# The output-gate tiles of a sink attention, multiplied between its steps

## The chip, the cores and the metric

The kernel runs on one core of one Trainium2 chip. The metric is the device time of one execution in microseconds, as the median of several executions; lower is better. Engines are named as the profile names them: PE is TensorE (PEld its weight loads), DVE is VectorE, ACT is ScalarE, SP is SyncE, which issues the DMA transfers.

## The reference, cut to what matters

Two transformer blocks follow each other on 256 tokens of width 1024. The second one puts 16 meta tokens ahead (272 positions) and starts with a gated attention with a sink logit for each head; the part that the change touches is this:

```python
def attention_mixer(h, norm_w, w_in, q_norm_w, k_norm_w, sinks, w_out):
    u = rms_norm(h, norm_w) @ w_in
    q, k, v, gate = jnp.split(
        u, [ATTN_WIDTH, ATTN_WIDTH + ATTN_KV_WIDTH, ATTN_WIDTH + 2 * ATTN_KV_WIDTH], axis=-1)
    q = rms_norm(q.reshape(B, L, ATTN_HEADS, ATTN_HEAD_DIM), q_norm_w)
    k = rms_norm(k.reshape(B, L, ATTN_KV_HEADS, ATTN_HEAD_DIM), k_norm_w)
    o = banded_sink_attention(q, k, v, sinks)
    return (o * jax.nn.silu(gate)) @ w_out
```

There are 16 query heads of 64 and 2 key/value heads. Everything is fp32.

## The kernel before, in words

The kernel is a sequence of stages, each a block of instruction streams written out by hand for PE, DVE, ACT and SP. An engine runs its stream in order, streams wait for each other by counting semaphores, and all engines meet at the end of a block. Weights come as tiles of 128x1024 fp32 into a ring of four buffers (`load_tiles`, on SP). Each tile is split in two parts for the products: `make_high` (ACT, L172) rounds it, `make_low` (DVE, L184) takes the rest; both parts have two buffers. `tile_T` multiplies one tile into a PSUM bank with 16 matmuls on the high part (L219) and 8 on the low part (L223), each 128x128 by 272 columns.

The stages around the change, in order of time:

- `project_T` for `attn_t`: 19 tiles, one after another on PE. Tiles 0 to 7 are the queries, 8 and 9 the keys, 10 the values, and 11 to 18 the output gate. DVE copies products 0 to 10 out of PSUM; ACT takes the eight gate products out with Silu (L1738) into `T2[:, 10:18]`.
- `value_rows_stage`: three PE transposes of the values, copied out by DVE (L1717).
- `head_norm_stage`, the norm of each query and key head; `meta_attention_stage`, the attention of the 16 meta tokens.
- `sink_attention_stage`: 16 units, u = 0 to 15, each two heads of one query tile of 128; units 0 to 7 see 144 keys, units 8 to 15 see 272. PE runs, in step u: `scores(u+2)` (L1509), `values(u-1)` (L1534), `turn(u)` (L1521, which transposes the probabilities). DVE runs, in its step u: `peaks(u)` (L1558 to L1571, the scores with bias into SBUF and their maximum), `scale(u-1)` (L1577, L1579, L1582, the probabilities divided by their sum, which `turn(u-1)` waits for) and `store(u-3)` (L1589, the product of `values` times the gate, into `y2`). ACT runs `exps(u)` (L1609, L1612) and `copy_turned(u-1)` (L1620, L1623), which `values(u-1)` waits for. `values` has PSUM banks 6 and 7 in turn. In step 2 ACT and DVE also split the first two tiles of `attn_out`.
- `out_rows` for `attn_out`: ACT and DVE split `y2` in pairs of rows (L2516, L2524), PE multiplies (L2547).

The same kernel has a stage of this kind in its first block, `attention_stage`, where weight tiles are multiplied between the steps of an attention; there `store` is on ACT.

## Time and profile before

| | |
|---|---|
| median of the runs (lowest to highest), us | 2078.43 (2077.08 to 2081.27) |
| the profiled execution, us | 2075.18 |
| its span, first to last instruction, us | 2073.4 |
| busy in the span: PE, DVE, ACT | 87%, 61%, 42% |
| mean granted clock of TensorE | 0.904 of 2.4 GHz |

A window of the trace gives the busy time of each engine in a stretch, and PEclk, the granted share of the full clock: 1.00 is 2.4 GHz and 0.50 is 1.2 GHz. A timeline gives start, duration, engine, line, operation and its operands, and in brackets how long the engine had been idle before and who released it. A fp32 matmul of this kernel shows as two records, so "x4" of L1509 are two matmuls.

### The profile page before, as it was taken

How to read it: one execution, taken by the hardware profiler on the slowest of the kernel's cores; microseconds unless marked ns; L12 is line 12 of the kernel's file. 1: busy time of each engine (PE TensorE's matmuls, PEld its weight loads, DVE VectorE, ACT ScalarE, POOL GpSimd, SP SyncE). 2: the span in 40 equal slices, each digit the busy share in tenths (PEclk: the TensorE clock that was granted, in tenths of full speed). 3: DMA queues.
4: the chain of work that ended last, by engine and by line, in shares of the span. 5: the costliest groups of instructions: out<-in, count | busy, mean ns of one | idle time of the engine just before them, and what ended most of it. 6: DMA issues, size and time to landing. Idle time of an engine off the chain costs nothing. (4 is left out here: it accounts for less than half of the span.)

```text
span 2073.4 us, 33110 instructions
## 1 busy us (share of the span) xinstructions
PE 1810.1 (87%) x11956; PEld 1612.6 (78%) x11956; DVE 1256.3 (61%) x2175; ACT 873.7 (42%) x1655; POOL 40.4 (2%) x24
## 2 busy tenths in 40 slices
PE   6899878899999986679999996869869887888878
PEld 6887768899999975668888885844568885888876
DVE  4544555589894459985555555546357634556554
ACT  3334543244444445545555554324334342234333
POOL 0000000000000000000000000000013200000000
PEclk9979989999999997769999998876889996999989
DMA  5422244455555530005666654410224430000014
GB/s 175 161 97 67 72 133 143 142 173 182 182 167 188 182 122 0 0 31 193 192 192 192 192 193 136 153 41 1 71 76 149 144 101 0 1 1 1 1 39 145
DMA packets 62765, 229.62 MB, mean 111 GB/s; under 512 B 6976, under 2 KB 7232, under 8 KB 62544
## 3 DMA queue, kind: packets, MB, share of 16 engines
q1 hardware_dynamic: 62672, 228.36, 34.1%
q8 instruction: 61, 1.00, 0.2%
q14 instruction: 32, 0.26, 0.0%
HBM read 227.29 MB, written 1.05 MB: 110 GB/s over the span
## 5 line engine op out<-in xcount | busy, mean ns | idle before, releaser
L981 DVE TENSOR_TENSOR tile_low<-weights,tile_high 128x1024 fp32r<-128x1024 f32 x252 | 307.4, 1223 | 248.0 <-ACT tile_high L971 243.0
L184 DVE TENSOR_TENSOR tile_low<-weights,tile_high 128x1024 fp32r<-128x1024 f32 x154 | 191.7, 1251 | 249.1 <-ACT tile_high L172 195.2
L971 ACT ACTIVATE tile_high<-weights 128x1024 fp32r<-128x1024 f32 x252 | 266.3, 1057 | 174.8 <-issue 173.7
L219 PE MATMUL banks<-parts,tile_high 128*128 128x272 f32 (+1 forms) x1904 | 270.7, 297 | 36.0 <-PEq L264 18.0
L219 PEld LDWEIGHTS banks<-parts,tile_high 128*128 128x128 f32 x1904 | 255.2, 200 | 43.6 <-issue 31.4
L172 ACT ACTIVATE tile_high<-weights 128x1024 fp32r<-128x1024 f32 x169 | 177.3, 1055 | 234.5 <-PE banks L219 100.1
L1025 PE MATMUL banks<-parts,tile_high 128*128 128x256 f32 x2048 | 268.6, 284 | 7.0 <-PEq L907 7.0
L1025 PEld LDWEIGHTS banks<-parts,tile_high 128*128 128x128 f32 x2048 | 256.9, 193 | 7.2 <-issue 7.2
L1312 PE MATMUL banks<-tile_high,parts 128*128 128x512 f32 x1024 | 255.1, 391 | 2.2 <-ACT parts L1292 2.2
L1312 PEld LDWEIGHTS banks<-tile_high,parts 128*128 128x128 f32 x1024 | 193.7, 189 | 42.7 <-issue 2.4
L1245 PE MATMUL banks<-rows 128*128 128x128 f32 x512 | 107.8, 378 | 48.6 <-ACT rows L1232 48.6
L1030 PE MATMUL banks<-parts,tile_low 128*128 128x256 f32 x1024 | 145.7, 285 | 3.0 <-DVE tile_low L981 3.0
L1245 PEld LDWEIGHTS banks<-rows 128*128 128x128 f32 x512 | 93.4, 274 | 63.0 <-issue 53.7
L223 PE MATMUL banks<-parts,tile_low 128*128 128x272 f32 (+1 forms) x952 | 140.3, 290 | 2.2 <-POOL tile_low L184 0.7
L1312 PE MATMUL banks<-tile_low,parts 128*128 128x512 f32 x512 | 137.7, 391 | 0.0
L1030 PEld LDWEIGHTS banks<-parts,tile_low 128*128 128x128 f32 x1024 | 132.6, 193 | 4.6 <-DVE tile_low L981 3.8
L1049 ACT ACTIVATE big<-banks 128x256 f32 (+1 forms) x127 | 49.0, 386 | 202.0 <-PE banks L1030 202.0
L223 PEld LDWEIGHTS banks<-parts,tile_low 128*128 128x128 f32 x952 | 127.8, 194 | 5.2 <-POOL tile_low L184 5.2
L1312 PEld LDWEIGHTS banks<-tile_low,parts 128*128 128x128 f32 x512 | 96.7, 189 | 20.2
L1232 ACT ACTIVATE rows<-rows 128x128 f32<-128x128 f32 x256 | 81.8, 390 | 72.3 <-DVE rows L1186 72.3
L2547 PE MATMUL banks<-tile_high,parts 128*128 128x512 f32 (+1 forms) x288 | 76.5, 413 | 10.9 <-ACT tile_high L172 9.5
L1186 DVE TENSOR_TENSOR rows<-const,rows 128x512 f32<-128x512 f32 x128 | 84.1, 714 | 1.4 <-PE banks L1245 1.1
(336 smaller groups left out, 2261.1 us busy)
## 6 DMA issues: line engine op xcount, KB each, us to landing
weights<-in_peer_u SPq DMA_DIRECT2D x128, 512.0 KB, 3.5
weights<-in_peer_v SPq DMA_DIRECT2D x128, 512.0 KB, 3.5
weights<-in_dn_qkv SPq DMA_DIRECT2D x32, 512.0 KB, 4.2
weights<-in_in_t SPq DMA_DIRECT2D x19, 512.0 KB, 3.6
weights<-in_attn_t SPq DMA_DIRECT2D x19, 512.0 KB, 3.5
weights<-in_in_m SPq DMA_DIRECT2D x16, 512.0 KB, 3.7
weights<-in_wq SPq DMA_DIRECT2D x16, 512.0 KB, 4.3
weights<-in_dn_z SPq DMA_DIRECT2D x16, 512.0 KB, 3.5
```

What stands on the lines that cost most here:

```text
L172: k.nc.scalar.activation(k.high[:, m % 2, :], k.ring.view(n), ACT.Copy).then_inc(*k.high_made.up())
L184: unit.tensor_tensor(k.low[:, m % 2, :], k.ring.view(n), k.high[:, m % 2, :].bitcast(F32), ALU.subtract).then_inc(*k.low_made[engine].up())
L219: ins = nc.tensor.matmul(out, high[:, c, :], rhs(c)[part], start=part + c == 0, stop=False)
L223: ins = nc.tensor.matmul(out, low[:, c, :], rhs(c)[0], start=False, stop=c == chunks - 1)
L971: k.nc.scalar.activation(k.high[:, (s + j) % 2, :], k.ring.buf[:, j % RING, :], ACT.Copy).then_inc(k.high_made.sem, 1)
L981: k.nc.vector.tensor_tensor(k.low[:, (s + j) % 2, :], k.ring.buf[:, j % RING, :], k.high[:, (s + j) % 2, :].bitcast(F32), ALU.subtract).th ...
L1025: ins = nc.tensor.matmul(ps[:, j, 0:S], high[:, c, :], x[:, c, :], start=part + c == 0, stop=False)
L1030: ins = nc.tensor.matmul(ps[:, j, 0:S], low[:, c, :], k.pair(S)[0][:, c, :], start=False, stop=c == KC - 1)
L1186: return nc.vector.tensor_tensor(out, iota.unsqueeze(1).broadcast_to([P, Q, NKEY]), choice(o, i, g, 0, Q).unsqueeze(2).broadcast_to([P, Q, ...
L1232: nc.scalar.activation(first[:, g % A, q, :], first[:, g % A, q, :], ACT.Copy, scale=choice(2, i, g, q, 1)).then_inc(scaled.sem, 1)
L1245: ins = nc.tensor.matmul(ps[:, g, q * P:(q + 1) * P], first[:, g % A, q, :], second[:, g % B, q, :], start=True, stop=True)
L1312: ins = nc.tensor.matmul(ps[:, 2 * tt + half, :], c[:, j % STAGES, tt * P:tt * P + P], v[:, half, :], start=head and j + part == 0, stop=t ...
```

## The change

The `attn_t` projection ends after tile 10. The eight gate tiles become a group `attn_g` of the ring, and each of the first eight steps of the sink attention multiplies one of them into PSUM bank 7; `values` keeps to bank 6 until these are through. Their first two splits are made in `value_rows_stage`, the others and the first two of `attn_out` in the attention, one in a step. ACT copies each gate product out, and in its step 10 applies Silu to all eight at once (2176 elements in a row). DVE's `store` becomes a plain copy. It belongs to step u-2 and stands ahead of `scale`. `out_rows` multiplies the rows by the gate, on DVE, ahead of splitting them (`open_gate`).

```diff
--- before.py
+++ after.py
@@ -38,6 +38,7 @@
 PH, TOPK = 8, 16
 NKEY = 128
 AH = 16
+N_ATTN = 11
 DNK, DNV = 8, 16
 CH = 64
 AHEAD = 2
@@ -119,7 +120,9 @@
     for j in range(NKEY):
         r.add(d["peer_v"][j])
     r.align()
-    for name in [n for n in ("attn_t", "attn_out", "dn_qkv", "dn_ba", "dn_z", "dn_out") if n in d]:
+    group("attn_t", d["attn_t"][0:N_ATTN])
+    group("attn_g", d["attn_t"][N_ATTN:])
+    for name in ("attn_out", "dn_qkv", "dn_ba", "dn_z", "dn_out"):
         group(name, d[name])
     k.tiles["end"] = len(r.slots)
@@ -1480,7 +1483,13 @@
     AK, GATE = 8, 10
     scored, masked, peaked, exped = k.start("att_scored", "att_masked", "att_peaked", "att_exped")
     scaled, turned, unturned, summed = k.start("att_scaled", "att_turned", "att_copied", "att_valued")
-    stored, stats = k.start("att_stored", "att_stats")
+    stored, stats, gated = k.start("att_stored", "att_stats", "gate_made")
+    fills = AH // 2
+    gate_tile = lambda i: k.tiles["attn_g"] + i
+    ahead = [gate_tile(i) for i in range(AHEAD, fills)] + list(early(k, "attn_out"))
+    high, low = k.pair(L)
+    fill = ps[:, 7, 0:L]
+    value_bank = lambda u: 6 + u % 2 if u > fills else 6
     units = [(tt, a) for tt in range(NT) for a in range(AH // 2)]
     keys = lambda tt: META + (tt + 1) * P
     soft, pt = k.soft2, k.pt2
@@ -1525,13 +1534,15 @@
             def values(u):
                 tt, a = units[u]
                 pe.wait_ge(*unturned.at(u + 1))
-                if u >= 2:
-                    pe.wait_ge(*stored.at(u - 1))
+                if u == fills + 1:
+                    pe.wait_ge(*gated.at(fills))
+                elif u:
+                    pe.wait_ge(*stored.at(u - 1 if u > fills else u))
                 tiles = key_tiles(tt)
                 for j in range(2):
                     g = (2 * a + j) // 8
                     for i, (_, n) in enumerate(tiles):
-                        ins = nc.tensor.matmul(ps[HD * j:HD * j + HD, 6 + u % 2, 0:P], k.v2[0:n, i, g * HD:(g + 1) * HD],
+                        ins = nc.tensor.matmul(ps[HD * j:HD * j + HD, value_bank(u), 0:P], k.v2[0:n, i, g * HD:(g + 1) * HD],
                                                pt[0:n, u % 2, i, j, :], start=i == 0, stop=i == len(tiles) - 1)
                 ins.then_inc(*summed.up())
@@ -1540,6 +1551,10 @@
             for u in range(len(units) + 1):
                 if u + 2 < len(units):
                     scores(u + 2)
+                if u < fills:
+                    if u:
+                        pe.wait_ge(*gated.at(u))
+                    tile_T(pe, k, gate_tile(u), fill, lambda c: (high[:, c, :], low[:, c, :]))
                 if u:
                     values(u - 1)
                 if u < len(units):
@@ -1586,19 +1601,17 @@
                 tt, a = units[u]
                 dve.wait_ge(*summed.at(u + 1))
                 cols = slice(META + tt * P, META + tt * P + P)
-                nc.vector.tensor_tensor(k.y2[:, a, cols], ps[:, 6 + u % 2, 0:P], T[:, GATE + a, cols],
-                                        ALU.mult).then_inc(*stored.up())
-
-            for u in range(len(units) + 3):
+                nc.vector.tensor_copy(k.y2[:, a, cols], ps[:, value_bank(u), 0:P]).then_inc(*stored.up())
+
+            for u in range(len(units) + 2):
                 if u < len(units):
                     peaks(u)
+                if u >= 2:
+                    store(u - 2)
                 if 1 <= u <= len(units):
                     scale(u - 1)
-                if u == 2:
-                    for n in early(k, "attn_out"):
-                        make_low(dve, k, n)
-                if u >= 3:
-                    store(u - 3)
+                if 1 <= u <= len(ahead):
+                    make_low(dve, k, ahead[u - 1])
 
         @block.scalar
         def _(act):
@@ -1628,17 +1641,23 @@
             for u in range(len(units) + 1):
                 if u < len(units):
                     exps(u)
+                if 1 <= u <= len(ahead):
+                    make_high(act, k, ahead[u - 1])
+                if 1 <= u <= fills:
+                    act.wait_ge(k.ring.used.sem, gate_tile(u - 1) + 1)
+                    nc.scalar.activation(T[:, GATE + u - 1, :], fill, ACT.Copy).then_inc(*gated.up())
                 if u:
                     copy_turned(u - 1)
-                if u == 2:
-                    for n in early(k, "attn_out"):
-                        make_high(act, k, n)
+                if u == fills + 2:
+                    act.wait_ge(*gated.at(fills))
+                    nc.scalar.activation(T[:, GATE:GATE + fills, :], T[:, GATE:GATE + fills, :],
+                                         ACT.Silu).then_inc(*gated.up())
 
 
 def meta_attention_stage(k):
 
     nc, ps, T = k.nc, k.ps, k.T2
-    AK, GATE = 8, 10
+    AK = 8
     pe_done, vec, exped = k.start("meta_product", "meta_vector", "meta_exped")
     m = META
     k.meta_soft, k.meta_turned = k.carve(k.mid, (AH, META), (AH, META))
@@ -1689,8 +1708,7 @@
             dve.wait_ge(*pe_done.at(2))
             done(nc.vector.tensor_copy(turned.rearrange("p h n -> p (h n)"), ps[0:m, 2, 0:AH * m]))
             dve.wait_ge(*pe_done.at(3))
-            done(nc.vector.tensor_tensor(k.y2[:, :, 0:m], ps[:, 3, 0:8 * m].rearrange("p (c n) -> p c n", c=8),
-                                         T[:, GATE:GATE + 8, 0:m], ALU.mult))
+            done(nc.vector.tensor_copy(k.y2[:, :, 0:m], ps[:, 3, 0:8 * m].rearrange("p (c n) -> p c n", c=8)))
 
         @block.scalar
         def _(act):
@@ -1715,6 +1733,13 @@
             for i, (_, n) in enumerate(spans):
                 dve.wait_ge(*turned.at(i + 1))
                 nc.vector.tensor_copy(k.v2[0:n, i, :], ps[0:n, i, 0:P]).then_inc(*copied.up())
+            for n in early(k, following):
+                make_low(dve, k, n)
+
+        @block.scalar
+        def _(act):
+            for n in early(k, following):
+                make_high(act, k, n)
 
 
 def second_block(k, stop):
@@ -1732,13 +1757,12 @@
     end_early(k, "attn_t")
     V = 10
 
-    def put(eng, i, src):
-        if i <= V:
-            return nc.vector.tensor_copy(k.vT2 if i == V else k.T2[:, i, :], src)
-        return nc.scalar.activation(k.T2[:, i - 1, :], src, ACT.Silu)
-    project_T(k, "attn_t", 19, L, (lambda i: "vector" if i <= V else "scalar", put), k.tiles["attn_out"] + RING)
+    project_T(k, "attn_t", N_ATTN, L,
+              (lambda i: "vector", lambda eng, i, src: nc.vector.tensor_copy(k.vT2 if i == V else k.T2[:, i, :], src)),
+              k.tiles["attn_g"] + RING)
     spans = [(0, META)] + [(META + tt * P, P) for tt in range(NT)]
-    value_rows_stage(k, spans)
+    value_rows_stage(k, spans, "attn_g")
+    end_early(k, "attn_g")
     if stop <= 22: return
 
     def apply_qk(c, wide):
@@ -1755,7 +1779,7 @@
     end_early(k, "attn_out")
     if stop <= 24: return
     out_rows(k, "attn_out", [(k.hm, 0, META, 0)] + [(k.h[:, tt, :], 2 + 2 * tt, P, META + tt * P) for tt in range(NT)],
-             k.y2, k.tiles["dn_qkv"] + RING)
+             k.y2, k.tiles["dn_qkv"] + RING, k.T2[:, 10:18, :])
     if stop <= 25: return
     deltanet(k, tiles, stop)
@@ -2494,12 +2518,12 @@
     peer(k, stop)
 
 
-def out_rows(k, name, tiles, x, prefetch):
+def out_rows(k, name, tiles, x, prefetch, gate=None):
 
 
     nc, ps, first = k.nc, k.ps, k.tiles[name]
     pairs, cols = x.shape[1] // 2, x.shape[2]
-    x_high, x_low, added = k.start("lhs_high", "lhs_low", "rows_added")
+    x_high, x_low, added, gated = k.start("lhs_high", "lhs_low", "rows_added", "lhs_gated")
     place = lambda q: slice(2 * (q % 4), 2 * (q % 4) + 2)
     high_x, low_x = k.pair(cols)
     with nc.Block() as block:
@@ -2513,16 +2537,26 @@
             for q in range(pairs):
                 if q >= 4:
                     act.wait_ge(k.ring.used.sem, first + 2 * (q - 4) + 2)
+                if gate is not None:
+                    act.wait_ge(*gated.at(q + 1))
                 nc.scalar.activation(high_x[:, place(q), :], x[:, 2 * q:2 * q + 2, :], ACT.Copy).then_inc(*x_high.up())
                 for half in range(2):
                     make_high(act, k, first + 2 * q + half)
 
         @block.vector
         def _(dve):
+            def open_gate(q):
+                if gate is not None and q < pairs:
+                    pair = x[:, 2 * q:2 * q + 2, :]
+                    nc.vector.tensor_tensor(pair, pair, gate[:, 2 * q:2 * q + 2, :], ALU.mult).then_inc(*gated.up())
+
+            open_gate(0)
+            open_gate(1)
             for q in range(pairs):
                 dve.wait_ge(*x_high.at(q + 1))
                 nc.vector.tensor_tensor(low_x[:, place(q), :], x[:, 2 * q:2 * q + 2, :],
                                         high_x[:, place(q), :].bitcast(F32), ALU.subtract).then_inc(*x_low.up())
+                open_gate(q + 2)
                 for half in range(2):
                     make_low(dve, k, first + 2 * q + half)
             dve.wait_ge(k.ring.used.sem, first + 2 * pairs)
```

Here is one step of DVE's stream in the units with 272 keys: in the order before, line L1577 to L1582 are `scale(u-1)`, L1589 is `store(u-3)`, and L1558 begins the next `peaks`. Names in brackets are the semaphores waited for.

```order
L1563 TENSOR_REDUCE small<-big 128x2 [waits att_stats,att_masked]
L1565 TENSOR_TENSOR small<-small,param 128x2 [waits att_stats]
L1568 TENSOR_TENSOR small<-param,small 128x2 [waits att_stats]
L1571 TENSOR_SCALAR small<-small 128x2 [waits att_stats]
L1577 TENSOR_TENSOR small<-small 128x2 [waits att_exped]
L1579 RECIPROCAL small<-small 128x2 [waits att_stats]
L1582 TENSOR_SCALAR big<-big,small 128x272 [waits att_stats]
L1582 TENSOR_SCALAR big<-big,small 128x272
L1589 TENSOR_TENSOR big<-banks,big 128x128 [waits att_valued]
L1558 SCALAR_TENSOR_TENSOR big<-big,banks 128x272 [waits att_turned,att_scored]
```

In the changed kernel `scale` is L1592 to L1597, `store` L1604.

```order
L1578 TENSOR_REDUCE small<-big 128x2 [waits att_stats,att_masked]
L1580 TENSOR_TENSOR small<-small,param 128x2 [waits att_stats]
L1583 TENSOR_TENSOR small<-param,small 128x2 [waits att_stats]
L1586 TENSOR_SCALAR small<-small 128x2 [waits att_stats]
L1604 COPY big<-banks 128x128 [waits att_valued]
L1592 TENSOR_TENSOR small<-small 128x2 [waits att_exped]
L1594 RECIPROCAL small<-small 128x2 [waits att_stats]
L1597 TENSOR_SCALAR big<-big,small 128x272 [waits att_stats]
L1597 TENSOR_SCALAR big<-big,small 128x272
L1573 SCALAR_TENSOR_TENSOR big<-big,banks 128x272 [waits att_turned,att_scored]
```

The store has moved from behind `scale` to ahead of it, and it is now that of unit u-2: its wait on `att_valued` is for the `values` that ran one step later than before.

PE's stream in the early steps, before: `values(u-1)` (L1534), `turn(u)` (L1521), `scores(u+3)` (L1509).

```order
L1534 MATMUL banks<-big 64x128 [waits att_stored,att_copied]
L1534 MATMUL banks<-big 64x128 x3
L1521 MATMUL banks<-const,big 16x128 [waits att_copied,att_scaled]
L1521 MATMUL banks<-const,big 16x128
L1521 MATMUL banks<-const,big 128x128 x2
L1509 MATMUL banks<-big 128x144 [waits att_masked]
L1509 MATMUL banks<-big 128x144
```

In the changed kernel (`values` L1545, `turn` L1530, `scores` L1518, a gate tile L222 and L226):

```order
L1545 MATMUL banks<-big 64x128 [waits att_stored,att_copied]
L1545 MATMUL banks<-big 64x128 x3
L1530 MATMUL banks<-const,big 16x128 [waits att_copied,att_scaled]
L1530 MATMUL banks<-const,big 16x128
L1530 MATMUL banks<-const,big 128x128 x2
L1518 MATMUL banks<-big 128x144 [waits att_masked]
L1518 MATMUL banks<-big 128x144
L222 MATMUL banks<-parts,tile_high 128x272 [waits high_made,gate_made]
L222 MATMUL banks<-parts,tile_high 128x272 x15
L226 MATMUL banks<-parts,tile_low 128x272 [waits low_made_vector]
L226 MATMUL banks<-parts,tile_low 128x272 x7
```

The 24 matmuls of a tile stand between `scores` and the next `values`, and wait for the copy of the gate product before (`gate_made`) and for the tile's splits.

ACT's stream in its step 10 has the Silu with a table load on either side; L1633 and L1636 are `copy_turned(9)`, L1622 begins `exps(11)`.

```order
L1633 ACTIVATE big<-banks 16x256 [waits att_valued,att_turned]
L1636 ACTIVATE big<-banks 128x512 [waits att_meta_copied]
L1653 ACT_TABLE_LOAD
L1653 ACTIVATE big<-big 128x2176 [waits gate_made]
L1622 ACT_TABLE_LOAD
L1622 ACTIVATE small<-small 128x2 [waits att_peaked]
```

The load and Silu of before stood at the first gate product of the projection; now they stand between a `copy_turned` and the next `exps`, and the load for Exp follows.

## Rows read from the trace of the kernel before

**Rows 1.** Windows; busy time by engine, PEclk is the granted share of 2.4 GHz

```profile
1301.46:1361.43 59.97, 59.97 (x456) 59.75 (x456) 24.70 (x28) 21.55 (x25) 0.00 (x0) 0.95 0.53 167
1410.00:1440.00 30.00, 28.54 (x104) 14.61 (x106) 19.80 (x84) 11.64 (x48) 0.00 (x0) 0.50 0.00 1
1440.00:1458.60 18.60, 16.87 (x110) 10.04 (x108) 15.10 (x55) 9.97 (x35) 0.00 (x0) 0.98 0.01 1
1458.60:1475.18 16.58, 11.88 (x49) 7.37 (x49) 2.14 (x9) 4.80 (x13) 0.00 (x0) 0.58 0.00 0
```

**Rows 2.** Timeline of PE in the projection; start and duration in us

```profile
1301.46 3.97 PE L219 MATMUL banks<-parts,tile_high 128*128 128x272 f32 x16 [6.21 <-PEq L264]
...
1307.04 2.39 PE L219 MATMUL banks<-parts,tile_high 128*128 128x272 f32 x16
...
1358.27 2.16 PE L219 MATMUL banks<-parts,tile_high 128*128 128x272 f32 x16
```

**Rows 3.** Timeline of PE, the attention's first instructions and its step 4

```profile
1394.41 2.31 PE L1509 MATMUL banks<-big 64*128 64x144 f32 x12 [0.94 <-PEq L1648]
...
1416.49 0.85 PE L1509 MATMUL banks<-big 64*128 64x144 f32 x4
1417.44 2.54 PE L1534 MATMUL banks<-big 16*64 16x128 f32 x8
1419.90 1.02 PE L1521 MATMUL banks<-const,big 128*16 128x128 f32 x4
```

**Rows 4.** Timeline of DVE, step 6 of its loop, scale(5)

```profile
1418.89 0.15 DVE L1577 TENSOR_TENSOR small<-small 128x2 f32<-128x2 f32 x1
...
1419.28 0.50 DVE L1582 TENSOR_SCALAR big<-big,small 128x144 f32<-128x144 f32 x2
```

**Rows 5.** Timeline of PE, turn(12), values(12), turn(13), full clock

```profile
1453.99 0.82 PE L1521 MATMUL banks<-const,big 128*16 128x128 f32 x6
...
1455.91 1.95 PE L1534 MATMUL banks<-big 16*64 16x128 f32 x12 [0.43 <-ACT big L1623]
1457.79 0.82 PE L1521 MATMUL banks<-const,big 128*16 128x128 f32 x6
```

**Rows 6.** Timeline of PE, values(13), turn(14), values(14)

```profile
1459.70 2.33 PE L1534 MATMUL banks<-big 16*64 16x128 f32 x12 [1.09 <-ACT big L1623]
1461.96 1.45 PE L1521 MATMUL banks<-const,big 128*16 128x128 f32 x6
1464.50 3.39 PE L1534 MATMUL banks<-big 16*64 16x128 f32 x12 [1.09 <-ACT big L1623]
```

**Rows 7.** Timeline of DVE, scale(15), store(13), store(14), store(15)

```profile
1460.78 0.16 DVE L1577 TENSOR_TENSOR small<-small 128x2 f32<-128x2 f32 x1 [1.98 <-ACT big L1612]
...
1461.18 0.63 DVE L1582 TENSOR_SCALAR big<-big,small 128x272 f32<-128x272 f32 x2
1462.07 0.29 DVE L1589 TENSOR_TENSOR big<-banks,big 128x128 f32<-128x128 f32 x1 [0.26 <-PE banks L1534]
1467.93 0.29 DVE L1589 TENSOR_TENSOR big<-banks,big 128x128 f32<-128x128 f32 x1 [5.57 <-PE banks L1534]
1473.79 0.29 DVE L1589 TENSOR_TENSOR big<-banks,big 128x128 f32<-128x128 f32 x1 [5.57 <-PE banks L1534]
```

**Rows 8.** Timeline, the turning of the value rows and what follows

```profile
1362.47 0.68 DVE L1717 COPY big<-banks 16x128 f32<-16x128 f32 x3 [5.64 <-PE banks L1711]
1363.44 0.75 ACT L1444 ACTIVATE big<-big 128x272 f32<-128x272 f32 x2 [1.58 <-PEq L1706]
```

**Rows 9.** By line: table load and split of one tile; duration ns min/median/max

```profile
L1738 ACT ACT_TABLE_LOAD  x1: 1283/1283/1283, 1340.6 to 1340.6; - x1
...
L172 ACT ACTIVATE tile_high<-weights x8: 1045/1060/1060, 1339.5 to 1406.3; 128x1024 fp32r<-128x1024 f32 x8
...
L184 DVE TENSOR_TENSOR tile_low<-weights,tile_high x8: 1218/1226/1227, 1406.4 to 1501.9; 128x1024 fp32r<-128x1024 f32 x8
```

**Rows 10.** Windows in the first block's attention, whose weight tiles lie between steps

```profile
225.00:230.00 5.00, 4.00 (x32) 3.76 (x32) 3.41 (x4) 2.96 (x7) 0.00 (x0) 1.00 0.15 43
```

More of the change, by code:

```diff
@@ L1699, in _, with value_rows_stage @@
             nc.scalar.activation(soft, soft, ACT.Exp).then_inc(*exped.up())
-def value_rows_stage(k, spans):
+def value_rows_stage(k, spans, following):
     nc, ps = k.nc, k.ps
```

## The prediction

> **What bounds the kernel now.** I read the windows by stage first. In the projection PE is busy all 59.97 us and its clock is full but for the beginning [rows 1]; DVE and ACT have less than half of that to do. So each tile costs PE its own time. The first runs at half clock and takes 1307.04 - 1301.46 = 5.58 us; the next seventeen take (1358.27 - 1307.04) / 17 = 3.01 us each [rows 2]. The attention, from 1394.41 [rows 3] to the end of the last store at 1473.79 + 0.29 = 1474.08 [rows 7], takes 79.7 us. It has three phases. From 1410 to 1440 PE is busy 28.54 of 30 us, at the half clock throughout; then 16.87 of 18.6 us at 0.98 of the full clock; then, once no scores are left, 11.88 of 16.58 us and mostly at half clock again [rows 1]. So it is PE's for most of the time, and its clock is set by something other than PE being busy.
>
> The timelines say what stands between PE's instructions. `turn(u)` needs `scale(u)` of DVE. Before the change this is nearly free: scale(5) runs from 1418.89 to 1419.78 [rows 4] while PE is in values(3), and turn(4) starts at 1419.90 [rows 3] with its own scale long done. DVE is one unit ahead of PE. That lead is what I follow below.
>
> **The change, part by part.**
>
> *The projection.* Eight tiles of 3.01 us go, on an engine that does nothing else: **-24.1 us**. The copies or Silus of their products lay beside PE. No transfer is late for it: DMA has 0.53 of its time taken there [rows 1].
>
> *The value rows.* Two tiles are now split there. DVE ends its copies at 1363.15 and the next stage starts at 1363.44 [rows 8]. ACT's two splits (1.06 us each) lie beside the copies for the most part, DVE's two (1.23 each) [rows 9] come behind the copies: **+2.5 us**, with no cover, since the block ends with them.
>
> *The attention's steps with a tile.* Here the first thing is the new wait. PE runs values(u-1), then turn(u). turn(u) waits for scale(u). DVE now has store(u-1) in its stream ahead of scale(u), and store(u-1) waits for values(u-1). So after each `values` PE has to wait for a store and a whole scale. That chain cannot be hidden by anything in PE's stream, because values(u-1) and turn(u) are neighbours in it. Its length, from rows: 0.04 from the end of `values` to the store (1459.70 + 2.33 = 1462.03 to 1462.07 [rows 6, 7]); the store 0.29 (as a plain copy perhaps a little less; I keep 0.29, and half of it would take 0.15 off each step); 0.05 to the next instruction; scale, 1418.89 to 1419.78, 0.89 with 144 keys [rows 4], or 1460.78 to 1461.81, 1.03 with 272 keys [rows 7]; 0.15 from there to `turn` (1461.96 [rows 6]). That is **1.42** and **1.56 us** in every step.
>
> The tile itself is 24 dense matmuls, 3.01 at full clock or 5.58 at half. No row has a dense tile within this attention, but the first block's has: over 225 to 230 PE is busy 4.00 of 5 us with gaps, and the clock stays at 1.00 [rows 10]. So I take the full clock once the first tile is through. The short instructions shrink with it: `values` is 1.95 at full and 3.39 at half clock for the same 12 records [rows 5, 6], a factor of 0.575, `turn` 0.82 against 1.45. For 144 keys this makes scores 0.85 to 0.48, values 2.54 to 1.46, turn 1.02 less its overlap to 0.55 [rows 3]. A step is then 0.48 + 3.01 + 1.46 + 1.42 + 0.55 = **6.9 us**. In it DVE has 0.89 + 0.29 + 1.23 for a split + some 1.6 for `peaks`, 4.0 in all, and ACT less: both are covered, and the splits are ready a step ahead.
>
> The start: three scores 2.31 [rows 3], the first tile 5.58 at half clock, turn and scores 0.95 each, the second tile 3.01, values 1.46, the wait 1.42: turn(1) starts 15.7 us into the stage. turn(7) is six steps on, 57.1. From there turn to values is 1.92 (1453.99 to 1455.91 [rows 5]; it is `copy_turned`, which no tile covers any more), values 1.46, the wait 1.56: turn(8) starts at **62.0**.
>
> *The steps without a tile.* Now turn, copy, values, store, scale, turn is one chain with nothing beside it. At full clock: 1.92 + 1.95 + 1.56 = 5.43 us, where the step before the change was 1457.79 - 1453.99 = 3.80 [rows 5]. At half: 2.54 (1461.96 to 1464.50) + 3.39 + 1.56 = **7.49** [rows 6]. Which clock? In a step of 5.43 PE works 1.95 + 0.82 and some 0.73 for scores, 3.5 us or 64%. The clock fell in the stretch from 1458.6 on, with two idle times of 1.09 us between the last steps and PE busy 72% [rows 1, 6]. I take it that it falls here too, after about two steps, and stays down, as it did over the last two steps of before. Seven steps: 2 x 5.43 + 5 x 7.49 = 48.3. The end: 2.54 to values, 3.43 to its store (1464.50 to 1467.93), 0.29 [rows 6, 7], 6.3. The stage lasts 62.0 + 48.3 + 6.3 = 116.6 us, 79.7 before: **+36.9 us**.
>
> *Silu in ACT's step 10.* Two loads of 1.28 and 2176 elements at the rate of a split (1.06 per 1024) [rows 9], 2.2: 4.8 us. ACT's own work in a step is about 9.97 / 18.6 x 3.80 = 2.0 us [rows 1], so a step of 7.49 leaves 5.5: **0**. Without that cover, in a step of 5.43, it delays copy_turned(10) by 1.4 us. The Trainium skill, "ScalarE: Activation LUTs", section "What ACT_TABLE_LOAD costs", puts a switch of table at about 2.66 us with a drain; by that the piece is 7.5 us and would show by 2.0 even in the slow step, for a sum of 18 in place of 16. The row of the load in this trace shows 1.283 us; I keep to it.
>
> *The head of `out_rows`.* The first multiplication of two rows by their gate is 544 elements on DVE; between 0.29 for 128 [rows 7] and 1.23 for 1024 [rows 9] that is **+0.7 us** ahead of ACT's first split. The others lie beside PE's products.
>
> *Sum*: -24.1 + 2.5 + 36.9 + 0 + 0.7 = **+16.0 us**. On the profiled execution, 2075.18, this is 2091.2; the median stands 3.25 higher, and I give **2094.5**. All other stages stay as they are.
>
> **The rivals.**
>
> *The clock stays full in the attention (12%).* For it: it held at 4.00 of 5 us with gaps in the first block [rows 10]. Against it: there dense tiles run on, here they have ended. Then seven steps of 5.43 and an end of 1.92 + 1.99 + 0.29: 62.0 + 38.0 + 4.2 + 1.4 (Silu) = 105.6, +25.9 for the stage and +5.0 in all: 2083.5. The Trainium skill, "TensorE: Matmul & The Clock Gate", Part 1, has the engine at 2.4 GHz when it is kept busy and at 1.2 GHz after idling; by that rule the steps here, busy for most of their time, would keep the full clock, and the time would be this 2083.5. The window of 1410 to 1440, 95% busy at 0.50 [rows 1], does not agree with so simple a rule.
>
> *The clock falls between the tiles too (15%).* From the end of one tile to the next there are 3.9 us in which PE is idle for 1.42, about the share at which it fell before. If half of each tile ran at the half clock, a step would be 1.3 us longer: six steps 8 us, and with all seven steps without a tile at half clock (+4.1) the sum is +28: 2106.
>
> *The new wait is not felt (5%); this one ends faster.* If DVE came to each store only after `values` had ended anyway, the wait would have no price. Its place is between `values` and `turn` in each step; it decides if DVE's own work of a step is as long as PE's. Then a step with a tile is 5.5, one without 3.8 as before: 15.7 - 1.4 + 6 x 5.5 + 3.4 + 7 x 3.8 + 4.2 + 1.4 = 82.9, +3.2 for the stage, -17.7 in all: 2060.7. Against it: scale(u) must follow the store in any case, so at least 1.03 + 0.15 stay; and DVE has 4.0 us of work in a step of 6.9.
>
> *The tiles are worth what they cost (8%).* The pieces are each a bit shorter (a store of 0.15, no idle before the first tile, a clock that comes back now and then), and the sum lands within 0.2% of before: 2075 to 2082.
>
> **How the numbers follow.** The forecast has 60%; within it the number of steps at full clock moves the sum by 2.06 each, 0 to 5 of them, 2088 to 2098.6. The range reaches down to the full clock (2083) and up to near the falls between tiles: **2083 to 2105**. No change that can be measured is about 0.2%, 4 us. Faster 0.05, same 0.09 (the near-even case and a little of the first rival), slower 0.86.
>
> **What would show it.** Right: a projection of 11 tiles, 24 us shorter; PE idle for about 1.4 to 1.6 us ahead of each `turn`, released by DVE's scale; DVE idle ahead of each store until `values` ends; steps of 6.9 us, then 5.4 to 7.5; PEclk near 1.00 in the first part and near 0.5 in the second. Wrong: `turn` starts right behind `values`, or PEclk stays at 1.00 to the end, or the tiles take over 3.01 each.

## The result, and the profile after

The changed kernel takes 2098.3 us (median; 2095.6 to 2100.6), against 2079.9 for the kernel before over the same rounds. The ratio is 1.0093, 95% interval 1.0072 to 1.0113: slower by 0.9%, 18 to 19 us, where +16.0 was forecast. The profiled execution took 2098.6 us, its span is 2096.8, 23.4 more than that of before. That is more than the medians differ by, because the profiled execution of before, 2075.2, is 4.7 us under its kernel's median.

Taken between the first matmuls of the stages on PE, that difference lies here:

| stretch | before | after | difference | forecast |
|---|---|---|---|---|
| projection of `attn_t` | 60.71 | 36.78 | -23.93 | -24.1 |
| value rows | 1.76 | 4.29 | +2.53 | +2.5 |
| head norm and meta attention | 30.48 | 32.31 | +1.83 | 0 |
| sink attention, to the first product of `out_rows` | 80.77 | 122.04 | +41.27 | +36.9 and +0.7 |
| everything ahead of and behind them | 1899.7 | 1901.4 | +1.7 | 0 |

In the windows of the changed kernel, the first is the projection, then head norm and meta attention, the sink attention from turn(1) to turn(7), and from turn(8) to its end. PEclk is the column behind POOL. [rows 1] has the same of before.

```profile
1301.58:1338.36 36.78, 35.98 (x264) 35.79 (x265) 15.07 (x20) 9.54 (x9) 0.00 (x0) 0.92 0.48 158
1342.65:1374.96 32.31, 21.36 (x140) 10.70 (x141) 12.49 (x28) 5.93 (x13) 0.00 (x0) 0.61 0.00 1
...
1388.16:1434.40 46.24, 39.12 (x241) 30.92 (x241) 21.72 (x73) 18.67 (x54) 0.00 (x0) 0.89 0.18 58
1438.71:1497.00 58.29, 43.13 (x164) 25.60 (x165) 21.24 (x75) 20.01 (x52) 0.00 (x0) 0.52 0.01 3
```

Of the 1.7 us in the last row of the table, 1.0 lie in the first tile of the output projection (6.56 us in place of 5.55) and 0.6 in that of the projection after it (5.58 in place of 4.97): the mean clock over them is 0.60 and 0.50 of the full one, where it was 0.73 and 0.58 before. PE is now busy for 39 of 46 us, and for 43 of 58; before it was 28.5 of 30 and 16.9 of 18.6 [rows 1]. The last stretch is at half clock almost throughout.

The timeline of PE in the steps with a tile (L222 and L226 are the tile, L1545 values, L1530 turn):

```profile
1388.16 0.60 PE L1530 MATMUL banks<-const,big 128*16 128x128 f32 x4 [1.19 <-DVE big L1597]
1388.70 0.52 PE L1518 MATMUL banks<-big 64*128 64x144 f32 x4
1389.14 3.61 PE L222 MATMUL banks<-parts,tile_high 128*128 128x272 f32 x16
1392.56 1.39 PE L226 MATMUL banks<-parts,tile_low 128*128 128x272 f32 x8
1393.87 1.51 PE L1545 MATMUL banks<-big 16*64 16x128 f32 x8
1396.57 1.02 PE L1530 MATMUL banks<-const,big 128*16 128x128 f32 x4 [1.19 <-DVE big L1597]
...
1405.43 0.52 PE L1518 MATMUL banks<-big 64*128 64x144 f32 x4
1405.88 2.26 PE L222 MATMUL banks<-parts,tile_high 128*128 128x272 f32 x16
```

Each `turn` from turn(1) on stands behind an idle time of 1.19 us that ends with L1597, the scale. The high part of a tile takes 2.26 us at full clock and 3.61 where part of it runs at half: the steps from one turn to the next, from turn(0) to turn(7), are 6.87, 8.41, 8.33, 6.87, 6.89, 7.11 and 8.63 us. The same on DVE, L1604 the store and L1592 to L1597 the scale:

```profile
1395.42 0.29 DVE L1604 COPY big<-banks 128x128 f32<-128x128 f32 x1 [4.67 <-PE banks L1545]
1395.63 0.15 DVE L1592 TENSOR_TENSOR small<-small 128x2 f32<-128x2 f32 x1
1395.81 0.17 DVE L1594 RECIPROCAL small<-small 128x2 f32<-128x2 f32 x1
1396.01 0.50 DVE L1597 TENSOR_SCALAR big<-big,small 128x144 f32<-128x144 f32 x2
```

DVE has sat idle for 4.67 us, released by `values` (which ends at 1393.87 + 1.51 = 1395.38), and only then does the scale run whose input had been there since 1391.8, when ACT's `exps` ended. PE and DVE take turns. In the steps without a tile:

```profile
1452.48 1.45 PE L1530 MATMUL banks<-const,big 128*16 128x128 f32 x6 [1.32 <-DVE big L1597]
1453.86 1.28 PE L1518 MATMUL banks<-big 64*128 64x272 f32 x4
1455.07 3.39 PE L1545 MATMUL banks<-big 16*64 16x128 f32 x12
1459.78 1.45 PE L1530 MATMUL banks<-const,big 128*16 128x128 f32 x6 [1.32 <-DVE big L1597]
```

A step is 7.30 us; the one at full clock before was 3.80 [rows 5].

Outside the attention's steps, these are the first products of the head norm (L1452, L1455) and of the output projection, before and then after:

```profile
1363.93 5.72 PE L1452 MATMUL banks<-big 128*20 128x272 f32 x20 [1.27 <-ACT big L1444]
1475.18 4.31 PE L2547 MATMUL banks<-tile_high,parts 128*16 128x512 f32 x12 [1.43 <-ACT parts L2516]
```

```profile
1342.65 7.96 PE L1455 MATMUL banks<-big 128*20 128x272 f32 x20 [3.79 <-ACT big L1447]
1497.00 5.28 PE L2581 MATMUL banks<-tile_high,parts 128*16 128x512 f32 x12 [2.21 <-ACT parts L2542]
```

### The profile page after: what moved, and what is told of

Its sections match the earlier page's. It is cut to its first block and busy times, and to the rows that moved or that the text cites. A ratio compares the mean times of both kernels' runs of the same rounds, so it can differ in the third digit from the quotient of the medians.

```text
span 2096.8 us, 33115 instructions
## 1 busy us (share of the span) xinstructions
PE 1819.8 (87%) x11956; PEld 1621.1 (77%) x11956; DVE 1258.0 (60%) x2179; ACT 876.2 (42%) x1656; POOL 40.4 (2%) x24
## 5 line engine op out<-in xcount | busy, mean ns | idle before, releaser
L222 PE MATMUL banks<-parts,tile_high 128*128 128x272 f32 (+1 forms) x1904 | 276.6, 301 | 36.1 <-PEq L267 18.0
L222 PEld LDWEIGHTS banks<-parts,tile_high 128*128 128x128 f32 x1904 | 260.0, 203 | 45.5 <-issue 32.7
L226 PE MATMUL banks<-parts,tile_low 128*128 128x272 f32 (+1 forms) x952 | 141.3, 292 | 2.2 <-POOL tile_low L187 1.0
L226 PEld LDWEIGHTS banks<-parts,tile_low 128*128 128x128 f32 x952 | 129.0, 196 | 5.2 <-POOL tile_low L187 5.2
```

The costliest lines, as they stand in the source:

```text
L222: ins = nc.tensor.matmul(out, high[:, c, :], rhs(c)[part], start=part + c == 0, stop=False)
L226: ins = nc.tensor.matmul(out, low[:, c, :], rhs(c)[0], start=False, stop=c == chunks - 1)
```

## The experiments

Each ratio is to the kernel before, on the same chip and in the same rounds, with its 95% interval. There are two sets, with a median of 2076.7 us for the kernel before in the first (store behind the scale, store alone, dense products, Silu last) and 2082.0 in the second (the others, and Silu last again). A difference of two ratios is less sure across sets, and less sure than its last digit throughout.

**The store behind the scale again.** In the changed kernel, DVE's loop:

```diff
-                if u >= 2:
-                    store(u - 2)
                 if 1 <= u <= len(units):
                     scale(u - 1)
+                if u >= 2:
+                    store(u - 2)
```

> The changed kernel with one thing undone: in each step of DVE the store of unit u-2 stands behind scale(u-1) again and no longer ahead of it; the tiles stay between the steps. Chain theory: turn starts right behind values, the steps with a tile take 5.6 us (6.9 to 8.6 in the changed kernel), those without 3.8 (7.3), the clock stays near 1.00, the Silu in ACT's step 10 now delays some 2.8 us; the attention takes about 82 us instead of 120, and the time is about 2060, 0.9% under the kernel before. Rival, the cost lies in the tiles themselves or in a clock that falls whatever stands between them: steps stay at 6.5 to 8 us and the time stays above 2085.

Measured: ratio 0.9972 (0.9951 to 0.9994), median 2070.8, single executions from 2064 to 2079. In PE's timeline only turn(8) still waits for DVE (1.56 us), and the steps with a tile take 5.6 us:

```profile
1404.90 0.60 PE L1530 MATMUL banks<-const,big 128*16 128x128 f32 x4
1405.43 0.52 PE L1518 MATMUL banks<-big 64*128 64x144 f32 x4
1405.88 2.27 PE L222 MATMUL banks<-parts,tile_high 128*128 128x272 f32 x16
...
1410.53 0.60 PE L1530 MATMUL banks<-const,big 128*16 128x128 f32 x4
...
1435.10 0.73 PE L1518 MATMUL banks<-big 64*128 64x272 f32 x4
1439.21 3.39 PE L1545 MATMUL banks<-big 16*64 16x128 f32 x12 [3.38 <-ACT big L1636]
1442.53 1.45 PE L1530 MATMUL banks<-const,big 128*16 128x128 f32 x6
```

The attention, to the first product of `out_rows`, is 88.4 us in place of 122.0. The late steps are 3.80, but for two: PE waits 3.38 us for ACT's copy behind the Silu, and the next one is at half clock, 8.18 and 4.55 us. So the chain was the cost, some 25 us of time by the two ratios. The expectation went too far by the rest: these two steps together are 5.1 us longer than two of 3.80, not 2.8, and against the kernel before the gain is 6 us, not 19. The profiled execution is one of the fast ones of this kernel (2066.3), so where the slower ones lose theirs isn't in a trace.

**The order of the store alone, in the kernel before.**

```diff
-            for u in range(len(units) + 3):
+            for u in range(len(units) + 2):
                 if u < len(units):
                     peaks(u)
+                if u >= 2:
+                    store(u - 2)
                 if 1 <= u <= len(units):
                     scale(u - 1)
...
-                if u >= 3:
-                    store(u - 3)
```

> The kernel before with only this taken from the change: DVE's store is that of unit u-2 and stands ahead of scale(u-1). No tile is moved, the gate is multiplied in the store as before. Chain theory: turn(u) waits for values(u-1), store and scale in every step; the early steps go from 4.37 to about 5.8 us, the late ones from 3.8 to about 7.3 at half clock; the time is about 2111 (+32), more than the changed kernel's, since nothing is saved in the projection. Rival, the wait falls into time in which PE is idle or DVE late anyway: under +5 us.

Measured: 1.0136 (1.0101 to 1.0171), median 2106.1, +28 by the ratio.

```profile
1418.09 1.02 PE L1521 MATMUL banks<-const,big 128*16 128x128 f32 x4 [1.18 <-DVE big L1582]
...
1423.71 1.02 PE L1521 MATMUL banks<-const,big 128*16 128x128 f32 x4 [1.19 <-DVE big L1582]
...
1454.40 1.45 PE L1521 MATMUL banks<-const,big 128*16 128x128 f32 x6 [1.32 <-DVE big L1582]
1455.78 1.28 PE L1509 MATMUL banks<-big 64*128 64x272 f32 x4
1456.99 3.39 PE L1534 MATMUL banks<-big 16*64 16x128 f32 x12
1461.69 1.45 PE L1521 MATMUL banks<-const,big 128*16 128x128 f32 x6 [1.32 <-DVE big L1582]
```

No tile has moved here, and the same 1.32 us and the same step of 7.29 us stand in the trace. The early steps went from 4.37 to 5.62 us. Here is one of 4.37, from the kernel before:

```profile
1415.54 1.02 PE L1521 MATMUL banks<-const,big 128*16 128x128 f32 x4
...
1419.90 1.02 PE L1521 MATMUL banks<-const,big 128*16 128x128 f32 x4
```

One reordering of DVE's stream accounts for the whole loss. Moving the tiles takes some 0.4% back from it; the two intervals just overlap, so that size is rough.

**Dense products in PE's wait.** In the changed kernel, five matmuls ahead of `turn(u)` for u from 8:

```diff
+            def warm(u):
+                bank = 7 if u <= fills + 1 else 6 + u % 2
+                ...
+                w = parts(k, k.tiles["attn_out"], 8)[0]
+                for c in range(5):
+                    nc.tensor.matmul(ps[:, bank, 0:L], w[:, c, :], high[:, c, :], start=True, stop=True)
...
                 if u:
                     values(u - 1)
+                if fills <= u < len(units):
+                    warm(u)
                 if u < len(units):
                     turn(u)
```

> The changed kernel with five dense matmuls (128x128 by 272 columns, into a free PSUM bank, their product is not used) on PE between values(u-1) and turn(u) in steps 8 to 15, where PE would wait for DVE's store and scale. The chain is not made shorter. If half of the late steps' price is the clock: PEclk stays near 1.00, the steps take 5.4 us instead of 7.3, the attention is 13 us shorter, the time about 2085. If the clock does not follow from PE's idle time here, or the fillers get in the way: 7.3 or more, time 2098 or above.

Measured: 1.0050 (1.0025 to 1.0075), median 2090.1, from 2082 to 2096. That is 9 us less than the changed kernel by the ratios, where 13 were expected; the two intervals just overlap, and the profiled execution is only 4.3 us shorter. In the trace the attention is 7.4 us shorter, but only 3.2 of it lie between turn(8) and turn(15), where the fillers are, and 1.4 in the last `values`; the rest is in the early steps, which are those of the changed kernel. The windows are turn(7) to values(11), then to turn(13), then to values(15):

```profile
1433.59:1462.87 29.28, 29.07 (x112) 18.22 (x112) 15.23 (x51) 13.94 (x35) 0.00 (x0) 0.54 0.00 1
1462.87:1471.45 8.58, 7.15 (x46) 4.70 (x45) 4.28 (x17) 3.18 (x11) 0.00 (x0) 0.98 0.00 1
1471.45:1487.87 16.42, 13.15 (x52) 8.88 (x53) 4.17 (x16) 4.12 (x11) 0.00 (x0) 0.58 0.00 1
```

PE is busy for 29.07 of 29.28 us and the clock is at half almost throughout; then it is full for two steps (5.97 and 5.19 us), in which PE is busy for less of the time, and falls again. At half clock the fillers end as the chain does and the step is 7.30 with or without them. So the clock is worth some 2 us in each late step (7.30 against 5.19), as the prediction had it, but PE's idle time alone doesn't explain its state: the mechanism of the first theory in the expectation fell.

**The store ahead in the steps with a tile only.** In the changed kernel:

```diff
-                if u >= 2:
+                if u >= 2 and u <= fills:
                     store(u - 2)
                 if 1 <= u <= len(units):
                     scale(u - 1)
+                if u > fills:
+                    store(u - 2)
```

> The changed kernel with the store behind scale only in DVE's steps from 9 on; in the steps with a tile it stays ahead, with its wait. Chain theory: steps 0 to 7 stay at 6.9 to 8.6 us, the steps without a tile fall from 7.3 to 3.8 at the full clock, with some 3 us for the Silu; some 21 us less than the changed kernel, about 2077. The difference to the run with the store behind scale throughout (13 us shorter again in its trace at most) is the price of the wait in the steps with a tile. Rival, the late steps are slow by the clock that the early ones leave behind: they stay above 5 us.

Measured: 1.0011 (0.9996 to 1.0026), median 2082.3, 17 us less than the changed kernel by the ratios where 21 were expected. With the first experiment and the changed kernel this divides the chain's price: about 0.8% for the steps without a tile (1.0093 to 1.0011) and 0.4% for those with one (1.0011 to 0.9972). The rival is half right in this trace: behind turn(8) the late steps have no wait for DVE, but three of the seven are at half clock and take 5.9 us, and the one with the Silu takes 8.05. The rows are turn(8) and turn(9), then a window from turn(7) into the last `values`.

```profile
1432.66 1.45 PE L1530 MATMUL banks<-const,big 128*16 128x128 f32 x6 [0.72 <-DVE big L1597]
...
1438.57 1.45 PE L1530 MATMUL banks<-const,big 128*16 128x128 f32 x6
```

```profile
1428.55:1476.00 47.45, 39.48 (x177) 23.48 (x178) 23.64 (x83) 21.23 (x56) 0.00 (x0) 0.67 0.00 1
```

**The Silu last.** As the first experiment, and in ACT's loop:

```diff
-                if u == fills + 2:
+                if u == len(units):
                     act.wait_ge(*gated.at(fills))
```

> As the run with the store behind scale, and with the Silu on the eight gate products moved from ACT's step 10 to behind its last copy, so that no load for Exp follows it. If the Silu and its two table loads (4.6 us on ACT) stop the short steps for want of cover: 1.5 to 3 us faster than that run, steps 10 to 12 all at 3.8 us, and up to 1 us of Silu sticks out at the end of the stage. If they are covered: no difference, or up to 1 us slower.

Measured in both sets: 0.9938 (0.9916 to 0.9961), median 2064.6, and again:

> The kernel with the store behind scale and Silu last, once more, beside the next two: 0.994 of the kernel before, as in its first run.

0.9927 (0.9904 to 0.9950), median 2064.2. The windows, of the first trace, are from the stage's start to turn(8), and from turn(8) to turn(15):

```profile
1376.21:1426.84 50.63, 48.71 (x333) 38.08 (x333) 32.82 (x112) 26.19 (x81) 0.00 (x0) 0.96 0.26 84
1426.84:1453.41 26.57, 22.24 (x147) 13.84 (x147) 19.34 (x71) 14.32 (x46) 0.00 (x0) 1.00 0.00 1
```

All seven late steps are 3.80 us at the full clock, with PE busy 84%; with the dense products in the wait it was at half with PE busy 99%. The gain over the first experiment is 0.3 to 0.5%, 7 to 9 us, more than the two slow steps of its trace account for (5.1, less 1.0 for the Silu at the end); the intervals of the first set overlap a little. At the end of the stage PE waits 3.19 us in place of 2.21 in the first of the two traces, which is the Silu sticking out by 1.0.

**The first two splits in the attention of the meta tokens.** On top of that, DVE and ACT of `meta_attention_stage`; the calls in `value_rows_stage` go:

```diff
+            for n in early(k, "attn_g"):
+                make_low(dve, k, n)
             dve.wait_ge(*pe_done.at(3))
...
             nc.scalar.activation(soft, soft, ACT.Exp).then_inc(*exped.up())
+            for n in early(k, "attn_g"):
+                make_high(act, k, n)
```

> As the kernel with Silu last, and the splits of the first two gate tiles are made in the attention of the meta tokens, where DVE waits 3.3 us for PE's last products, and no longer in the stage of the value rows. If these splits cost 2.5 us at the end of that stage and 1.8 more by a clock that has fallen before the head norm: 4 us faster than the kernel without this. If only the 2.5 us come back: 2.5. If the head norm is bound by ACT either way: 2.5 or less.

Measured: 0.9908 (0.9882 to 0.9935), median 2061.9. The interval overlaps that of the run before it, so the time doesn't decide. The trace decides the first piece: from the value rows to the head norm 1.77 us, as before the change, in place of 4.28. The second it leaves half open. The stretch of head norm and meta attention is 31.67 us here, 30.29 in the next kernel, and 32.3 to 32.6 in all six traces that have the splits in the value rows. Here are the norm's first products in this kernel, and in the next one (the changed kernel's took 7.96, behind 3.79 of idle time):

```profile
1338.63 7.09 PE L1455 MATMUL banks<-big 128*20 128x272 f32 x20 [1.27 <-ACT big L1447]
```

```profile
1337.52 5.72 PE L1455 MATMUL banks<-big 128*20 128x272 f32 x20 [1.27 <-ACT big L1447]
```

It was 5.72 before the change too. The two kernels have the same instructions up to here, so the norm's time follows the clock, and the clock may fall in it without the added idle time too. The late steps of this execution were at 0.60 of the full clock for a while (4.99, 5.90, 5.91 and 4.47 us), with the same instructions that ran at 1.00 above:

```profile
1421.57:1442.84 21.27, 20.83 (x88) 12.40 (x89) 12.09 (x44) 8.95 (x30) 0.00 (x0) 0.60 0.00 1
```

**The Silu in halves.** On top of that, four products behind the last copy but one and four behind the last:

```diff
-                if u == len(units):
+                if u >= len(units) - 1:
                     act.wait_ge(*gated.at(fills))
-                    nc.scalar.activation(T[:, GATE:GATE + fills, :], T[:, GATE:GATE + fills, :],
-                                         ACT.Silu).then_inc(*gated.up())
+                    half = slice(GATE + 4 * (u - len(units) + 1), GATE + 4 * (u - len(units) + 2))
+                    nc.scalar.activation(T[:, half, :], T[:, half, :], ACT.Silu).then_inc(*gated.up())
```

> As the run with the splits moved, and the Silu in two halves, behind the last but one and behind the last copy on ACT. The 1.0 us of Silu that stuck out at the end of the attention is then covered: 0.5 to 1.0 us faster than that run, and the first product of the output projection comes 2.2 us after the last values, not 3.2. If the first half delays the last copy: no gain.

Measured: 0.9930 (0.9903 to 0.9956), median 2066.3 over four executions, 2058 to 2069. Inconclusive in time. In the trace the piece came out as expected: the first product of the output projection comes 2.21 us after the last values.

```profile
1452.90 1.95 PE L1545 MATMUL banks<-big 16*64 16x128 f32 x12 [1.09 <-ACT big L1636]
1457.06 5.07 PE L2578 MATMUL banks<-tile_high,parts 128*16 128x512 f32 x12 [2.21 <-ACT parts L2539]
```

With the Silu last and whole it was 3.19 behind last values as short as these (1.95 us), and 2.21 only in the second trace, where they ran at half clock (3.13 us) and covered it.

## Why the prediction was right

The path was right, and the number is closer than its parts. By the traces the difference is 23.4 us and not 16.0: 3.7 more in the attention, 1.8 in head norm and meta attention, 1.7 elsewhere. The medians differ by 18.4 only because the profiled execution of before was a quick one; that part of the agreement is luck.

*The wait between values and turn* was the step that carried it, and it is shown: it is there in each step of the changed kernel, gone when the store goes behind the scale, and there again in the kernel before with nothing but the store moved. Its size was 1.19 and 1.32 us, not 1.42 and 1.56. Two terms were too long. The scale starts 0.21 us after the store has begun, where 0.29 + 0.05 were put. And from the scale's end to `turn` it is 0.06 (1396.01 + 0.50 = 1396.51 to 1396.57), where 0.15 was read from turn(14) at 1461.96 [rows 6, 7]: that turn starts right behind values(13) and wasn't waiting for its scale. The scale itself took what was put for it.

*The projection* (-24.1, measured -23.93) and *the value rows* (+2.5, measured +2.53) came out as forecast. So did *the head of `out_rows`*: between the last values and its first product PE was idle for 1.43 us before the change and for 2.21 after it (+0.8, forecast +0.7), and ACT's first split is now released by DVE's multiplication (L2551, begun at 1495.44).

*The steps with a tile.* 6.9 us came out for three of the seven, 6.87 to 6.89, and 7.11 for the first with longer scores; the other three, 8.3 to 8.6, had part of a tile at half clock. This is the rival in which the clock falls between the tiles. It was taken for 15% and an alternative; in the changed kernel's trace it is there for three steps of seven and costs 4.5 us, and PEclk is 0.89 over turn(1) to turn(7). Two errors cancel in the 6.9: the wait was 0.23 shorter than put, and a tile at full clock took 3.19 us here (1405.88 to 1409.07), not 3.01. So the sign of being wrong that names tiles of over 3.01 us did appear. The stage's start was 2.5 us shorter than worked out (turn(1) at 13.2, not 15.7), because the clock rose within the first tile, and turn(7) to turn(8) took 4.3 us and not 4.9. Turn(8) started 63.75 us into the stage, not 62.0.

*The steps without a tile.* 7.30 at half clock against 7.49 worked out, and one, not two, that ran partly at the full clock (6.47 from turn(8) to turn(9)): 50.2 us against 48.3.

*The Silu* was covered, as forecast: both loads took 1.28 us and the Silu 2.02, and the next copy on ACT still waited 0.44 us for PE:

```profile
1447.69 1.28 ACT L1653 ACT_TABLE_LOAD   x1
1448.99 2.02 ACT L1653 ACTIVATE big<-big 128x2176 f32<-128x2176 f32 x1
1451.02 1.28 ACT L1622 ACT_TABLE_LOAD   x1
...
1453.97 0.37 ACT L1633 ACTIVATE big<-banks 16x256 f32<-16x256 f32 x1 [0.44 <-PE banks L1530]
```

The instructions stand 0.01 to 0.02 us apart: the drain that "ScalarE: Activation LUTs" of the Trainium skill (section "What ACT_TABLE_LOAD costs") adds to a load does not show here, and the trace's 1.28 us is what a load cost. That the Silu is free only in slow steps is shown by the first experiment, where PE waited 3.38 us behind it and not 0.43.

*Where the reason was weaker than the number*: the clock. I argued that it falls in the late steps because PE is busy for 64% of them only. It did fall, and PE was busy 43 of 58 us. But it stayed at 1.00 in steps with PE busy 84%, was at 0.54 with PE busy 99%, and over the same first late steps, with the same instructions, it was at 1.00 in one kernel and at 0.60 in another. So the half clock in the late steps of the changed kernel is measured, its cause is not. It stays open: what was tried is the filling of PE's idle time; that the kind of product (transposes, products on 64 rows, dense tiles) has a part in it was not tested. The rule of the Trainium skill, "TensorE: Matmul & The Clock Gate" (Part 1), that a busy engine runs at the full clock, doesn't agree with the 0.54 either.

*What was missed*: +1.8 us in head norm and meta attention, put at nothing. The norm's first products took 7.96 us in place of 5.72, behind 3.79 us of idle time in place of 1.27. With the splits moved away that stretch was 31.67 us in one kernel and 30.29 in the next, so what the splits have to do with it is likely, not shown.

## What to carry to other kernels

When a wait is moved ahead in an engine's stream, look at what stands behind it there and who waits for that: here a store of 0.29 us, put ahead of a scale to free a PSUM bank sooner, tied PE and DVE together step by step and cost 25 us, more than the eight tiles took off the projection. Before such a move, check that the engine that reads the later work does not also feed the wait: here `values` fed the store, and `turn`, the next on PE, read the scale. Work moved into a stage that PE fills at half clock can still gain by what the clock gives: with the store behind the scale a step with a tile took 5.62 us and one without had taken 4.37, so a tile of 3.01 us cost 1.25. The clock that was gained shows in the instructions beside the tile: a `turn` took 0.60 us in that step and 1.02 before. The tiles alone were worth 0.3% with the Silu between the steps, and 0.6 to 0.7% with it behind them, where no step had to wait for it.

## What the runs showed of the hardware

- The granted clock of TensorE over the first four steps without a tile was 1.00 in one kernel and 0.60 in another whose steps were the same, the first products of a head norm took 5.72 and 7.09 us in two kernels that were the same up to them, and filling PE's idle time with dense products (PE busy 29.07 of 29.28 us) did not hold it (0.54).
- The kernel with a stall of 3.4 us in its late steps had a wide spread between executions, 2064 to 2079 us; the one without that stall took 2062 to 2068 in the same rounds, but 2061 to 2074 in the second set. So it isn't shown that the stall makes the spread, and what does was not traced.
- Short instructions on DVE start 0.18 to 0.21 us apart, whether the first is busy for 0.15 us and the next reads its result, or is a store of 0.29 us that the next does not need: a chain is read from starts, not summed from durations.
